# Attention pairs of a two-layer block: head norms from sums by token, first scores inside the next projection, weight splits among the softmax steps

## What is computed

```python
def forgetting_attention(q, k, v, f_logit, g_q, g_k):      # 16 heads of 64
    qn = rms_norm(q, g_q).transpose(0, 2, 1, 3)             # norm over the 64 of each head and token
    kn = rms_norm(k, g_k).transpose(0, 2, 1, 3)
    vh = v.transpose(0, 2, 1, 3)
    cum = jnp.cumsum(log_sigmoid(f_logit), axis=1).transpose(0, 2, 1)
    for blk in range(seq // 128):
        q0, q1 = blk * 128, blk * 128 + 128
        s = einsum("bhqd,bhkd->bhqk", qn[:, :, q0:q1], kn[:, :, :q1]) * HEAD_DIM ** -0.5
        s = s + cum[:, :, q0:q1, None] - cum[:, :, None, :q1]
        p = softmax(where(causal, s, -inf), axis=-1)
        outs.append(einsum("bhqk,bhkd->bhqd", p, vh[:, :, :q1]))
```

## Time and profile before

| what | value |
|---|---|
| time, median of 3 runs | 5052.97 us (5052.86 to 5055.14) |
| the profiled execution, its time | 5055.57 us |
| the profiled execution, its span | 5053.7 us |
| PE busy | 4573.9 us, 91% of the span |
| DVE busy | 2913.3 us, 58% |
| ACT busy | 1813.4 us, 36% |
| POOL busy | 591.5 us, 12% |
| mean granted clock of PE | 0.946 |

### The profile page before, as it was taken

One profiled execution on the slowest core, in us unless ns is written; L12 is line 12 of the kernel. 1 busy time (PEld: TensorE's weight loads), 2 busy tenths in 40 slices (PEclk: granted clock), 3 DMA queues, 4 the chain that ended last, 5 costly groups with the idle time before them and its releaser, 6 DMA issues.

```text
span 5053.7 us, 64730 instructions
## 1 busy us (share of the span) xinstructions
PE 4573.9 (91%) x22059; PEld 3844.3 (76%) x22059; DVE 2913.3 (58%) x4604; ACT 1813.4 (36%) x2888; POOL 591.5 (12%) x631
## 2 busy tenths in 40 slices
PE   8999988999999999889999887897546799999999
PEld 7887776778878877767788765686435799999998
DVE  5436556444254265664542684443899666666666
ACT  3225333332232254333322322232218544444444
POOL 0000000000000000000000000010575322222221
PEclk9999999999999999999999977798869999999999
DMA  3222210222222222102222210031003577777776
GB/s 123 100 100 76 92 50 33 75 85 98 100 92 91 100 84 84 58 33 72 87 99 100 73 71 1 17 125 42 34 33 133 210 277 277 278 275 274 278 277 241
DMA packets 85576, 599.86 MB, mean 119 GB/s; under 512 B 10640, under 2 KB 11024, under 8 KB 18512
## 3 DMA queue, kind: packets, MB, share of 16 engines
q1 hardware_dynamic: 57456, 410.85, 22.4%
q0 software_dynamic: 27136, 162.28, 9.1%
q10 hardware_dynamic: 864, 25.17, 1.2%
HBM read 570.99 MB, written 27.26 MB: 118 GB/s over the span
## 4 chain that ended last, share of the span: by engine, by line
PE 65%; issue 14%; DVE 11%; ACT 5%; DVEq 3%; ACTq 1%; DMA 1%; POOLq 0%; POOL 0%; SPq 0%
PE PB L188 19%; PE PB L190 19%; PE PB L189 19%; DVE RS L1201 2%; PE PB L895 2%; PE PB L1083 1%; PE PB L884 1%; PE PB L1916 1%; ACT STG L2355 1%; DVE PB L1800 1%; DVE WL L169 1%; DVE NM L915 1%; DVEq L1802 1%; DVEq L2214 1%; DVE SC L2217 1%
## 5 line engine op out<-in xcount | busy, mean ns | idle before, releaser
L188 PE MATMUL PB<-XH,WH 128*128 128x512 f32 (+1 forms) x3552 | 1352.2, 381 | 112.1 <-DVE WL L169 77.3
L189 PE MATMUL PB<-XL,WH 128*128 128x512 f32 (+1 forms) x3552 | 1339.1, 377 | 0.0
L190 PE MATMUL PB<-XH,WL 128*128 128x512 f32 (+1 forms) x3552 | 1338.5, 377 | 0.0
L169 DVE TENSOR_TENSOR WL<-RAW,WH 128x1024 fp32r<-128x1024 f32 x520 | 645.8, 1283 | 498.2 <-ACT WH L161 484.7
L188 PEld LDWEIGHTS PB<-XH,WH 128*128 128x128 f32 x3552 | 675.9, 190 | 234.8 <-issue 85.9
L189 PEld LDWEIGHTS PB<-XL,WH 128*128 128x128 f32 x3552 | 675.3, 190 | 108.1 <-issue 4.0
L190 PEld LDWEIGHTS PB<-XH,WL 128*128 128x128 f32 x3552 | 674.3, 190 | 101.8
L161 ACT ACTIVATE WH<-RAW 128x1024 fp32r<-128x1024 f32 x520 | 520.4, 1050 | 576.1 <-PE PB L190 551.4
L247 POOL TENSOR_TENSOR SQ<-SQ 128x512 f32<-128x512 f32 x49 | 71.7, 1464 | 2389.1 <-ACT SQ L230 2377.9
L188 PE MATMUL PB<-WH,WGH 128*128 128x512 f32 x768 | 299.7, 390 | 9.8 <-DVE WGL L2494 9.8
L190 PE MATMUL PB<-WH,WGL 128*128 128x512 f32 x768 | 302.1, 393 | 0.0
(11 more groups left out here) (393 smaller groups left out, 7593.8 us busy)
## 6 DMA issues: line engine op xcount, KB each, us to landing
RAW<-weights SPq DMA_DIRECT2D x387, 1024.0 KB, 4.8
gate_matrix<-STG ACTq DMA_DIRECT2D x6, 4096.0 KB, 11.5
GM<-gate_matrix POOLq DMA_DIRECT2D x128, 192.0 KB, 5.4
X<-x SPq DMA_DIRECT2D x4, 512.0 KB, 5.7
UV<-rows,IDX POOLq DMA_INDIRECT x128, 5.7
out<-FIN SPq DMA_DIRECT2D x4, 512.0 KB, 2.6
MEMX<-mem POOLq DMA_DIRECT2D x1, 1024.0 KB, 5.0
SK<-sub_keys POOLq DMA_DIRECT2D x1, 1024.0 KB, 5.1
```

The lines of the kernel that those rows point to most:

```text
L169: c.nc.vector.tensor_tensor(c.WL[p][:, cols], c.RAW[p][:, cols], c.WH[p][:, cols].bitcast(F32), ALU.subtract).then_inc(c.sem("w_split"), 1)
L188: c.nc.tensor.matmul(out, wh, xh, start=start, stop=False)
L189: c.nc.tensor.matmul(out, wh, xl, start=False, stop=False)
L190: return c.nc.tensor.matmul(out, wl, xh, start=False, stop=stop)
```

## The change

`pair_schedule` goes, and each engine's stream is written out, with a common loop `pair_rounds`.

- **Norm by token.** `head_sums` becomes `token_sums`: 8 matmuls with a 128x128 block of the squares as weights and two columns of ones by head as the moving operand, so that bank 6 holds 16 numbers for each token of a block. ACT takes roots of 128x16 (`R16`), DVE reciprocals of 128x16, and copies each 64 times into `RE` (128x1024). `spread` then multiplies `RE` (as weights) with the identity, 8 matmuls of 128 columns, which brings the factors back to one row for each channel in banks 6 and 7. ACT copies them to `SQ2` (`widen`), and DVE's `norm` takes them from there; the two masked copies of the forget terms come first.
- **Order on PE.** Pair i+2 is projected after the steps of pair i, not pair i+1 ahead of them. `spread` of pair i+1 stands within this projection ahead of slice 2, and the scores of steps 0 and 1 of pair i+1 stand ahead of slice 7. `token_sums` stands ahead of `turn`. The output's transposes go to bank 4, the tile after the gate tile to banks 6 and 7.
- **Splits and squares.** ACT does the two halves of a split after the exponentials of steps 1 and 2, and the squares after step 4; DVE does its halves at the end of rounds 2 and 3 of its step loop. The gate tile's successor is split in the last pair's steps.
- **Tables.** ACT does a dummy exponential of 128x1 (`exp_table`) after the outputs.

```diff
+def act_split(c, act, t, p, loads, halves=(0, 1)):
+    if 0 in halves:
+        act.wait_ge(c.sem(f"w_loaded{p}"), loads * 16 + 16)
+        act.wait_ge(c.sem("tile_done"), t + 1)
+    for half in halves:
...
+def dve_split(c, dve, t, p, halves=(0, 1)):
+    for half in halves:
...
-OWN_BANK = 4
+OWN_BANK = 6
...
-    scores(0)
-    scores(1)
+    if not begun:
+        pe_scores(c, pe, st, 0)
+        pe_scores(c, pe, st, 1)
     turn(0)
     for j in range(len(st.steps)):
-        scores(j + 2)
+        pe_scores(c, pe, st, j + 2)
...
         top(j + 2)
         if j + 1 < len(st.steps):
             copy(j + 1)
...
+        if between:
+            between(j)
...
+        if between:
+            between(j)
...
+def pair_rounds(eng, cur):
+    with eng.Fori(0, PAIRS // 2 - 1) as i:
+        for j in (0, 1):
+            yield i * 2 + j, [Tile(cur, i, j + n, 1) for n in range(3)]
...
+    def token_sums(i):
+        pe.wait_ge(c.sem("qk_sq"), base + i + 1)
+        for g in range(2):
+            for qb in range(QB):
+                at = (g * QB + qb) * 2
+                last = c.nc.tensor.matmul(c.PB[:, 6, at:at + 2], c.SQ2[:, g, qb * P:qb * P + P],
+                                          c.ONESB[:, 0:P:HD], start=True, stop=True)
+        last.then_inc(c.sem("qk_sum"), 1)
+    def spread(i):
+        pe.wait_ge(c.sem("qk_scale"), base + i + 1)
+        for g in range(2):
+            for qb in range(QB):
+                last = c.nc.tensor.matmul(c.PB[:, 6 + g, qb * P:qb * P + P],
+                                          c.RE[:, g, qb, :], c.IDENT[:, :],
+                                          start=True, stop=True)
+        last.then_inc(c.sem("qk_spread"), 1)
+    def turn(i):
+        pe.wait_ge(c.sem("o_ready"), base + i + 1)
         for qb in range(QB):
-            last = c.nc.tensor.transpose(c.PB[:, b + 1, qb * P:qb * P + P], c.OQ[:, qb, :], c.IDENT[:, :])
+            last = c.nc.tensor.transpose(c.PB[:, 4, qb * P:qb * P + P], c.OQ[:, qb, :], c.IDENT[:, :])
         last.then_inc(c.sem("ot_ready"), 1)
...
+    def project(t, p, b, i=None, st=None):
+        WH = c.WH[p][:, :].rearrange("p (k m c) -> p k m c", k=DC, m=2)
+        WL = c.WL[p][:, :].rearrange("p (k m c) -> p k m c", k=DC, m=2)
         for k in range(DC):
             if k in (0, DC // 2):
-                pe_half(c, pe, t.t, k // (DC // 2))
-            if k == DC // 2:
-                turn(i, b)
+                pe_half(c, pe, t, k // (DC // 2))
+            if st and k == 2:
+                spread(i)
+            if st and k == DC - 1:
+                pe.wait_ge(c.sem("qk_ready"), base + i + 1)
+                pe_scores(c, pe, st, 0)
+                pe_scores(c, pe, st, 1)
+            if i is not None and not st and k == DC // 2:
+                turn(i)
             for m in range(2):
-                last = mm3(c, c.PB[:, OWN_BANK + m, :], WH[:, k, m, :], WL[:, k, m, :], c.XH[:, k, :], c.XL[:, k, :],
+                last = mm3(c, c.PB[:, b + m, :], WH[:, k, m, :], WL[:, k, m, :], c.XH[:, k, :], c.XL[:, k, :],
                            k == 0, k == DC - 1)
         last.then_inc(c.sem("tile_done"), 1)
...
+    first, second = Tile(cur, 0, 0, 1), Tile(cur, 0, 1, 1)
+    pe.wait_ge(c.sem("ps_done"), first.n + 1)
+    project(first.t, first.p, first.b)
+    token_sums(0)
+    pe.wait_ge(c.sem("ps_done"), second.n + 1)
+    project(second.t, second.p, second.b, 0, steps(0, first.b))
+    for i, (own, _, ahead) in pair_rounds(pe, cur):
+        pe_steps(c, pe, steps(i, own.b), True)
+        token_sums(i + 1)
+        turn(i)
+        project(ahead.t, ahead.p, ahead.b, i + 1, steps(i + 1, 2 - own.b))
+    i = PAIRS - 2
+    own, last, gate = (Tile(cur, 0, i + n, 1) for n in range(3))
+    pe_steps(c, pe, steps(i, own.b), True)
+    token_sums(i + 1)
+    turn(i)
+    project(gate.t, gate.p, gate.b, i + 1, steps(i + 1, last.b))
+    pe_steps(c, pe, steps(i + 1, last.b), True)
+    project(gate.t + 1, gate.next_p, OWN_BANK, i + 1)
+    cur.t += PAIRS
+    cur.n += PAIRS
...
+        c.nc.scalar.activation(c.R16[:, :], c.PB[:, 6, :16], ACT.Sqrt,
+                               bias=c.EPSC[:, 0:1], scale=1.0 / HD).then_inc(c.sem("qk_root"), 1)
+    def widen(i):
+        act.wait_ge(c.sem("qk_spread"), base + i + 1)
+        for g in range(2):
+            c.nc.scalar.activation(c.SQ2[:, g, :], c.PB[:, 6 + g, :], ACT.Copy).then_inc(c.sem("qk_wide"), 1)
...
+    def exp_table():
+        c.nc.scalar.activation(c.EXPD[:, :], c.EPSC[:, 0:1], ACT.Exp)
...
+    def beside(tile, square):
+        def work(j):
+            if j in (1, 2):
+                act_next(c, act, tile, (j - 1,))
+            if j == 4 and square:
+                squares(tile)
+        return work
...
+    for i, (own, after, _) in pair_rounds(act, cur):
+        attend(i, beside(after, True))
+        roots(i + 1)
+        outputs(i)
+        exp_table()
+        widen(i + 1)
...
+    attend(i + 1, beside(gate, False))
...
+    def scale(i):
+        dve.wait_ge(c.sem("qk_root"), base + i + 1)
+        V.reciprocal(c.R16[:, :], c.R16[:, :])
+        dve.drain()
+        V.tensor_copy(c.RE[:, :, :, :].rearrange("p g q (h d) -> p (g q h) d", h=2),
+                      c.R16[:, :].unsqueeze(2).to_broadcast([P, 16, HD])).then_inc(c.sem("qk_scale"), 1)
     def norm(i, b):
-        dve.wait_ge(c.sem("qk_root"), base + i + 1)
-        V.reciprocal(c.RS2[:, :, :], c.RS2[:, :, :])
...
+        own, other = [slice(hh * HD, hh * HD + HD) for hh in range(2)], [slice(HD, P), slice(0, HD)]
+        col = PRM["g_k"][0]
...
+            V.tensor_scalar(c.QZ[hh][other[hh], :], c.CQ[other[hh], :], c.HMASK[other[hh], bass.ds(i * 2 + hh, 1)],
+                            None, ALU.mult)
+        dve.wait_ge(c.sem("qk_wide"), (base + i) * 2 + 1)
+        for hh in range(2):
+            V.scalar_tensor_tensor(out=c.QZ[hh][own[hh], :], in0=c.PB[own[hh], b, :], scalar=c.GQ8[own[hh], l, 0:1],
+                                   in1=c.SQ2[own[hh], 0, :], op0=ALU.mult, op1=ALU.mult)
+        dve.wait_ge(c.sem("qk_wide"), (base + i) * 2 + 2)
+        for hh in range(2):
+            last = V.scalar_tensor_tensor(out=c.KZ[hh][own[hh], :], in0=c.PB[own[hh], b + 1, :],
+                                          scalar=c.PR[own[hh], l, col:col + 1],
+                                          in1=c.SQ2[own[hh], 1, :], op0=ALU.mult, op1=ALU.mult)
         last.then_inc(c.sem("qk_ready"), 1)
...
+    def attend(i, b, tile):
+        def beside(j):
+            if j in (2, 3):
+                dve_next(c, dve, tile, (j - 2,))
+        dve_steps(c, dve, Steps((base + i) * 8, [{"nk": P * qb + P} for hh, qb in JS], (c.PM, c.PT, c.SUM)), beside)
...
+    for i, (own, after, _) in pair_rounds(dve, cur):
+        attend(i, own.b, after)
+        scale(i + 1)
+        outputs(i)
+        norm(i + 1, after.b)
...
-            c.SQ2, c.RS2 = c.sb("SQ2", [P, 2, S], F32, s), c.sb("RS2", [P, 2, S], F32, s)
+            c.SQ2, c.RE = c.sb("SQ2", [P, 2, S], F32, s), c.sb("RE", [P, 2, QB, P], F32, s)
...
+            c.R16, c.EXPD = c.sb("R16", [P, 16], F32, s), c.sb("EXPD", [P, 1], F32, s)
```

More of the change, by code:

```diff
@@ L170, in dve_split, with act_next, dve_next @@
                                   ALU.subtract).then_inc(c.sem("w_split"), 1)
[L173 to L178, removed]
+def act_next(c, act, tile, halves=(0, 1)):
+    act_split(c, act, tile.t + 1, tile.next_p, tile.next_loads, halves)
+def dve_next(c, dve, tile, halves=(0, 1)):
+    dve_split(c, dve, tile.t + 1, tile.next_p, halves)
 def pe_half(c, pe, t, half):
@@ L869, in blocks, with pe_scores, pe_steps @@
     return [(kb, min(P, nk - kb * P)) for kb in range((nk + P - 1) // P)]
[L872 to L878, removed]
+def pe_scores(c, pe, st, j):
+    if j < len(st.steps):
+        pe.wait_ge(c.sem("p_ready"), st.count + (j + 1))
+        st.steps[j]["scores"](c.PB[:, 6 + j % 2, :]).then_inc(c.sem("s_ready"), 1)
+def pe_steps(c, pe, st, begun=False):
     def turn(j):
@@ L906, in pe_steps, with dve_steps @@
         product(j)
-def dve_steps(c, dve, st):
+def dve_steps(c, dve, st, between=None):
     def top(j):
@@ L1070, in pe_attention, with steps @@
     pe_values(c, pe, cur, 3, c.XH, c.XL)
[L1072 to L1079, removed]
+    base = l * PAIRS
+    def steps(i, b):
         def step(hh, qb):
@@ L1175, in attend @@
+    def widen(i):
[4 more added lines that the diff above has]
+        c.nc.scalar.activation(c.EXPD[:, :], c.EPSC[:, 0:1], ACT.Exp)
+    def attend(i, after):
         act_steps(c, act, Steps((base + i) * 8, [{"nk": P * qb + P} for hh, qb in JS], (c.PM, c.PT, c.SUM),
-                                [qb * 2 + hh for hh, qb in JS]))
@@ L1178, in outputs @@
-    def outputs(i, b):
+                                [qb * 2 + hh for hh, qb in JS]), after)
+    def outputs(i):
         act.wait_ge(c.sem("ot_ready"), base + i + 1)
-        c.nc.scalar.activation(c.YH[:, i, :], c.PB[:, b + 1, :], ACT.Copy).then_inc(c.sem("ot_hi"), 1)
```

(59 more changed lines are left out.)

35 lines of the change are left out of this document (3 added, 32 removed).

## The result

The median of the kernel after is 5024.45 us (5023.38 to 5025.41, 4 runs), that of the kernel before, on the same chip, 5052.91 (5050.58 to 5055.14, 4 runs). The ratio is 0.9942, with a 95% interval of 0.9928 to 0.9957. The profiled execution took 5024.48 us with a span of 5021.6, against 5055.57 and 5053.7. From the first Square to the start of the last output copy of each layer, the pairs' part, the two layers together took 531.2 us before and 500.1 after, 31.1 less; the rest of the span was 4522.5 and 4521.5. The medians differ by 28.5 and the profiled executions by 31.1, since the profiled execution of the kernel before lies 2.7 above its median and that of the kernel after on it.

The account below looks back on a forecast made before the run. PE, busy 91% of the span, was taken to bound the kernel. Path -32.5 us and clock +5.6 gave -26.9: 5028.7 from the profiled 5055.57, about 5027 on the median's scale; 8-in-10 range 5008 to 5048.

Parts of the forecast that it names:

- The gaps: PE waits removed per pair: 1.16 us before first scores, 2.19 before first transposes, 0.92 before the output's transposes.
- The additions: Work added on PE's path per pair: token sums 1.64 us, `spread` 1.94, delays in the steps 0.3.
- Waits in the steps: Expected profile: PE waits about 1.5 us per pair within the steps, the largest before step 6's transposes.
- What is hidden: Norm's chain after token sums, about 2.2 us, runs under PE's transposes and two slices, with 1 us to spare.
- rival (d): Roots or `spread` come late, PE waits 1 to 2 us within each projection; 5043 to 5059 us; chance 0.08.
- (e): Splits and squares in the steps set the pace of maxima and exponentials; slower, up to 5109 us; chance 0.07.
- the two more switches per pair: Table loads on ACT if Square lay in another set: up to 85 us over 16 pairs; left out of the sum.
- The clock: PE's half-clock falls: 19 us before; one per pair after, 16 x 1.54 = 24.6 us, taking back 5.6.
- (a): Likeliest case: one clock fall in each pair; 5027 us, own range 5018 to 5036; chance 0.50.
- (b): Clock falls no more often than before, or less, as PE is dense; 5002 to 5019 us; chance 0.18.
- (c): Clock falls last twice as long, another 16 x 1.54; 5051 us, nearly no change; chance 0.15.
- the 7 that the prediction had named as a sign of being wrong: PE's clock staying low for 7 us on end would show the prediction wrong.

Follow-up runs that it names:

- e2: Changed kernel with both halves of each weight split taken out of the steps and put back between the pairs; 5013.18 us, ratio 0.9918 to the kernel before.
- e6: Kernel before with only the weight splits moved into the steps, norm and scores as they were; 5032.02 us, ratio 0.9953 to the kernel before.
- e3: Changed kernel with the scores of steps 0 and 1 issued behind the projection's last slice, not ahead; 5040.01 us, ratio 0.9971 to the kernel before.
- e1: Changed kernel with token sums of 128 columns in place of two, roots reading every 64th column; 5000.77 us, ratio 0.9894 to the kernel before.
- e10: Changed kernel with early splits and `spread` as PE transposes, token sums kept at two columns; 5011.17 us, ratio 0.9910 to the kernel before.
- e8: Changed kernel with 128-column token sums, splits out of the steps, and `spread` as PE transposes; 4980.87 us, ratio 0.9855 to the kernel before.
- e9: Changed kernel with 128-column token sums and `spread` as PE transposes, splits left in the steps; 4983.04 us, ratio 0.9855 to the kernel before.
- e5: Changed kernel with 128-column token sums and the weight splits taken out of the steps; 5002.31 us, ratio 0.9897 to the kernel before.

## Why the prediction was right

**The gaps.** All three went, as forecast: -1.16, -2.19, -0.92. For the second the reason was only partly right. I put it down to the splits leaving the place ahead of the maxima and to the earlier scores. e2 leaves the splits there and the gap stays away; what removes it is that DVE is through with the norm early enough to have the split done before the scores come. e6 shows that moving the splits does help as long as DVE is late. e3 sizes the place of the scores at 0.52.

**The additions.** Token sums 1.76 (forecast 1.64), `spread` 1.95 (1.94), steps 12.20 against 756.48 - 744.55 = 11.93, so +0.27 (0.3). Waits in the steps are 1.15 us per pair, not 1.5, and none stands out before step 6, where I looked for the largest. The full-clock period fell by 2.30, forecast 2.18; fourteen times that is 32.2, and with 2.0 for the last pairs, which is the forecast's figure and was not measured by itself, the path gave 34, where 32.5 was the forecast.

**What is hidden.** The chain of roots took 1.5 us from the last token sum, not 2.2, and met 3.3 us of cover, or some 1.8 without the half clock. No wait at `spread` or for `QZ` appears, so rival (d) did not come. Nor did (e): the splits and squares set the pace of nothing. The number of table loads in the pairs' part is unchanged, 16 for roots and 16 for exponentials, and none was made for a Square within the steps; so the two more switches per pair that the prediction worked out under the Trainium skill's rule (ScalarE: Activation LUTs, Table sets: the hidden batching unit), on the condition that Square lay in another set, did not occur.

**The clock.** Forecast: one fall in each of 16 pairs, 24.6 us, 5.6 more than before. Measured: 12 stretches, two of them double, none in the pairs around 846, 2164 and 2222 and none at the second layer's first sums, around 2041. Ten of 1.62 and two of 3.22 cost 22.6, 3.6 more than the 19. So path and clock, -34 and +3.6, give -30.6, and 31.1 were measured in the pairs' part. Both sums were off by 2 us or less, in the same direction. On the profiled execution's scale the forecast of 5028.7 is 4.2 above the 5024.48 measured; on the median's, 5027 is 2.6 above. (The prediction's own figures, 5028.7 less 2.6, make 5026.1, a slip of 1 us that changes nothing.) The mechanism, sums of two columns that thin out PE's work, was named rightly, and e1, and e10 against e8, show it. What I took too lightly is how much of it lies in the width: I held the transposes, products and waits in the steps to be as thin, and with wide sums and the splits in the steps they never brought the clock down (e1, e9); with the splits early they did so once in e5 and twice in e8. In the words of the rivals the outcome is (a) with a piece of (b), and double stretches, the form of (c), in two places. These lasted 6.8 us, just under the 7 that the prediction had named as a sign of being wrong.

That the number is so near is in part luck. Four missing stretches and two double ones make 14 lengths where 16 were forecast. Nothing in the working decides that count: with the same sums of two columns it was 11 in e2, 19 in e3 and 22 in e10, and each length is worth 1.6 us.

The Trainium skill's rule on transposes (TensorE: Matmul & The Clock Gate, Part 4: PE-mode transpose), by which the transposes would make the stretch emptier, does not show as harm here: e9, with eight transposes per projection in place of sixteen matmul records, has no time at half clock, and e8 has 6.8 us where e5, without them, has 3.4. They lie amid 512-column matmuls, so this does not test the rule where transposes stand alone.

**Left open.** Why some pairs fall and others, with the same instructions, don't, and why a stretch is sometimes double. What in the steps brings it down with wide sums and early splits is not known either. The dummy exponential of the change was never taken out by itself; e6, without it, keeps 1.10 us of gap where e3, with it, has 0.52, but the two differ in more than that. Sums between 2 and 128 columns wide were not tried, so where the change from falling to not falling lies is not known. The order of e1 and e5, and that of e8 and e9, is not settled: their medians differ by 2 us, no more than what the rest of the program varies by.

## What to carry to other kernels

A matmul that loads a fresh block of weights and moves two columns takes about as long as one that moves 128 (1.76 against 1.84 us for 16 here), and in this kernel the narrow ones brought TensorE's clock down to its lower level behind them: give such sums their full width if the output has room. Read the granted clock beside the busy share, since PE was busy 100% in every one of the stretches of the kernel after. And test the parts of a change against the whole: moving the splits gained 22 us alone and lost 10 inside the whole, 5 in the steps and 5 by the clock, because another part had already freed the engine whose lateness it cured.

## What the runs showed of the hardware

- Widening 16 matmul records from 2 columns to 128 cost 0.08 us and removed 47.8 us at half clock over 16 pairs, worth 22.7 us (e1 against the change); from e10 to e8 it removed 68.3 us of 75.1.
- A stretch at half clock cost 1.6 us where it lasted 3.4 and 3.2 where it lasted 6.8, in two kernels.
- A transpose of a 128x128 float32 block went as one record, 1.03 us for eight (0.12 apart), where the identity matmul took two, 1.95 us for eight.
- A reciprocal over 128x1024 took 6.55 us (kernel before) and over 128x16 0.25 (kernel after); a copy of 1024 with a repeated source, from the engine's memory to the same, 0.69 us, as long as a copy of 512 that reads PSUM.
- The table load of 1.28 us started ahead of the wait of the exponential that needs it (772.90, with the maxima at 774.99): hidden in the kernel before, it came onto the path in e6, when the wait got short.
